# The sample attention of a decoder step written anew: keys turned by VectorE, running sums, unrolled units

## What is computed

```python
z = jnp.einsum('bqhd,bkhd->bhqk', qb, kb, preferred_element_type=jnp.float32) * scale + bias
log_beta = jax.nn.log_sigmoid(z)
log_keep = jnp.where(mask, log_beta - z, 0.0)
rest = lax.cumsum(log_keep, axis=3, reverse=True) - log_keep
a = jnp.where(mask, jnp.exp(log_beta + rest), 0.0)
outs.append(jnp.einsum('bhqk,bkhd->bqhd', a.astype(vb.dtype), vb))
```

## Time and profile before

| | |
|---|---|
| median of 3 runs | 3729.41 us (3727.08 to 3733.83) |
| the profiled execution | 3737.79 us |
| its span, first to last instruction | 3736.1 us |
| mean granted clock of PE | 0.946 |
| PE busy | 3210.8 us (86%) |
| DVE busy | 1885.8 us (50%) |
| ACT busy | 937.8 us (25%) |
| POOL busy | 610.8 us (16%) |
| DMA packets | 432.70 MB, mean 116 GB/s |

### The profile page before, as it was taken

One profiled execution on the slowest core, in us unless ns is written; L12 is line 12 of the kernel. 1 busy time (PEld: TensorE's weight loads), 2 busy tenths in 40 slices (PEclk: granted clock), 3 DMA queues, 4 the chain that ended last, 5 costly groups with the idle time before them and its releaser, 6 DMA issues. The chain is left out here.

```text
span 3736.1 us, 57991 instructions
## 1 busy us (share of the span) xinstructions
PE 3210.8 (86%) x20912; PEld 2718.3 (73%) x20912; DVE 1885.8 (50%) x3138; ACT 937.8 (25%) x1598; POOL 610.8 (16%) x528
## 2 busy tenths in 40 slices
PE   5655999999995979788888887888885999999997
PEld 1235999999985979555555555444484999999996
DVE  2566555555543121344444444888815555555554
ACT  0113000000012010333333333777714100000003
POOL 0002222212101111122222221000010222222210
PEclk7887999999997989899999998999997999999998
DMA  8702111111101220798888886000010211111101
GB/s 323 261 29 62 46 45 45 40 43 42 39 0 58 88 63 26 284 351 341 337 350 334 340 339 225 22 19 23 6 45 0 68 45 45 45 45 45 45 22 48
DMA packets 215604, 432.70 MB, mean 116 GB/s; under 512 B 13664, under 2 KB 130057, under 8 KB 212441
## 3 DMA queue, kind: packets, MB, share of 16 engines
q1 hardware_dynamic: 215521, 431.67, 31.7%
HBM read 417.92 MB, written 13.92 MB: 116 GB/s over the span
## 5 line engine op out<-in xcount | busy, mean ns | idle before, releaser
L84 PE MATMUL bank<-hi,mlp_uphi 128*128 128x364 f32 (+1 forms) x1536 | 506.9, 330 | 92.2 <-POOL mlp_uplo L697 92.2
L85 PE MATMUL bank<-lo,mlp_uphi 128*128 128x364 f32 (+1 forms) x1536 | 506.7, 330 | 0.0
L86 PE MATMUL bank<-hi,mlp_uplo 128*128 128x364 f32 (+1 forms) x1536 | 506.6, 330 | 0.0
L85 PE MATMUL bank<-mlp_flo,mlp_dnhi 128*128 128x364 f32 (+1 forms) x1536 | 504.7, 329 | 0.0
L86 PE MATMUL bank<-mlp_fhi,mlp_dnlo 128*128 128x364 f32 (+1 forms) x1536 | 504.7, 329 | 0.0
L84 PE MATMUL bank<-mlp_fhi,mlp_dnhi 128*128 128x364 f32 (+1 forms) x1536 | 504.6, 329 | 0.0
L307 DVE SCALAR_TENSOR_TENSOR x_t<-bank,mod,x_t 128x364 f32<-128x364 f32 (+1 forms) x432 | 245.5, 571 | 379.7 <-PE bank L86 377.4
L84 PEld LDWEIGHTS bank<-hi,mlp_uphi 128*128 128x128 f32 x1536 | 290.5, 189 | 93.4 <-POOL mlp_uplo L697 93.4
L697 POOL TENSOR_TENSOR mlp_uplo<-mlp_raw,mlp_uphi 128x1024 fp32r<-128x1024 f32 x64 | 162.5, 2540 | 827.3 <-ACT mlp_uphi L682 423.3
L85 PEld LDWEIGHTS bank<-lo,mlp_uphi 128*128 128x128 f32 x1536 | 290.5, 189 | 0.0
L86 PEld LDWEIGHTS bank<-hi,mlp_uplo 128*128 128x128 f32 x1536 | 290.3, 189 | 0.0
(11 more groups left out here) (255 smaller groups left out, 5652.7 us busy)
## 6 DMA issues: line engine op xcount, KB each, us to landing
sa_kpage<-in_cache_k SPq DMA_DIRECT2D x256, 512.0 KB, 6.4
sa_vpage<-in_cache_v SPq DMA_DIRECT2D x256, 512.0 KB, 6.1
mlp_raw<-in_w_up SPq DMA_DIRECT2D x64, 512.0 KB, 4.0
mlp_raw<-in_w_down SPq DMA_DIRECT2D x64, 512.0 KB, 3.5
w_raw<-in_w_ada SPq DMA_DIRECT2D x24, 1024.0 KB, 8.6
pm_wada<-in_w_ada SPq DMA_DIRECT2D x48, 512.0 KB, 5.2
kv_raw<-in_w_kv SPq DMA_DIRECT2D x8, 1024.0 KB, 5.5
x_rows<-in_x_prompt SPq DMA_DIRECT2D x1, 4096.0 KB, 13.4
```

The costliest lines, as they stand in the source:

```text
L84: pe.matmul(out, w_hi, x_hi, start=start, stop=False, skip_group_check=True)
L85: pe.matmul(out, w_hi, x_lo, start=False, stop=False, skip_group_check=True)
L86: return pe.matmul(out, w_lo, x_hi, start=False, stop=stop, skip_group_check=True)
```

## The change

The 64 units of the 8 sequences are counted through as n = 0 to 63 and unrolled, without a hardware loop.

- Keys are turned by DVE, in 32x32 blocks and from SBUF to SBUF, one instruction a page. It does so two units ahead: the four turns of unit n+2 stand at the head of DVE's iteration n, and the softplus chain of unit n behind them.
- The scores are made by 128 matmuls a unit with 32x32 weights and 128 columns at 16 positions of the array, into four banks by row group.
- ACT, and no longer DVE, adds the bias: four activations.
- DVE keeps a running sum of the softplus over the pages (sa_crun) and splits that. Six matmuls a unit with neg_tri and neg_above subtract it; neg_ones goes.
- POOL only prepares each sequence's share of the new keys. The queries of the next sequence are laid out in units 2 to 5, and a sequence is finished in the next one's unit 1. The output has two banks.
- SP's waits count turned pages by unit. Its order is as before. The first two units of keys are let through at the stage's start.
- setup makes two constants fewer (neg_ones, mask_diag: four POOL operations), and places move.

```diff
@@ attend_sample: sync
-sp.wait_ge(k_turned, b * TURNS + (2 * (n + 25) if n < 8 else 2 * (n - 7) + TURNS))
+sp.wait_ge(turned, b * (4 * UNITS) + (4 * u - 4 + EARLY_K))
-    sp.wait_ge(v_used, b * UNITS + (u + 6))
+    sp.wait_ge(v_used, b * UNITS + (u - 2 + EARLY_V))
@@ attend_sample: scalar
+def softplus_of_negative(n):
+    act.wait_ge(z_done, n + 1)
+    act.wait_ge(zt_done, n)
+    for r in range(4):
+        act.activation(z_rows[:, :, r, :],
+                       Z[r][:, P * (n % 2):P * (n % 2) + P].rearrange("p (x j) -> p x j", j=32),
+                       ACT.Identity, bias=k.bias_row[:, 0:1]).then_inc(z_kept, 1)
+    act.wait_ge(zt_done, n + 1)
+    act.wait_ge(c_done, 4 * n)
+    act.activation(flat, ZT[n % 2][:, :], ACT.Abs).then_inc(abs_done, 1)
+    act.wait_ge(abs_done, n + 1)
+    act.activation(flat, flat, ACT.Exp, scale=-1.0).then_inc(e_done, 1)
+    act.wait_ge(e_done, n + 1)
+    act.activation(flat, flat, ACT.Ln, bias=1.0).then_inc(l_done, 1)
+
+softplus_of_negative(0)
+for n in range(W):
+    if n + 1 < W:
+        softplus_of_negative(n + 1)
+    act.wait_ge(tri_done, n + 1)
+    if n:
+        act.wait_ge(v_used, EARLY_V + n)
+    act.activation(att[:, :, :].rearrange("p g n -> p (g n)"), ZT[n % 2][:, :], ACT.Exp).then_inc(a_done, 1)
@@ attend_sample: vector
+dve.tensor_reduce(sp_all[:, :], sp_new[:, :, :].rearrange("p b n -> p n b"), AX.X, ALU.add).then_inc(summed, 1)
...
+dve.tensor_reduce(att_all[:, :], att_new[:, :, :].rearrange("p b n -> p n b"), AX.X, ALU.add
+                  ).then_inc(summed, 1)
...
+def turn_keys(n, x):
+    if n >= W:
+        return
+    if x == 0:
+        if n >= 2:
+            dve.wait_ge(z_done, n - 1)
+    dve.wait_ge(k_in[4 * (n % 2) + x], 16 * (n // 2 + 1))
+    dve.transpose(k_t[n % 2][:, x, :], k_raw[n % 2][:, x, :]).then_inc(turned, 1)
...
+for n in range(2):
+    for x in range(4):
+        turn_keys(n, x)
+for n in range(W):
+    b, u = divmod(n, UNITS)
+    for x in range(4):
+        turn_keys(n + 2, x)
+    flat = t[:, :, :].rearrange("p g n -> p (g n)")
+    dve.wait_ge(l_done, n + 1)
+    dve.scalar_tensor_tensor(flat, ZT[n % 2][:, :], 0.0, flat, ALU.max, ALU.add).then_inc(sp_done, 1)
+    dve.wait_ge(sp_done, n + 1)
+    if n:
+        dve.wait_ge(lo_done, n)
+    for g in range(4):
...
+        dve.tensor_tensor(c_run[:, g, :], before, t[:, g, :], ALU.add).then_inc(c_done, 1)
+    c_all = c_run[:, :, :]
+    dve.wait_ge(c_done, 4 * n + 4)
+    if n:
+        dve.wait_ge(tri_done, n)
+    dve.tensor_copy(c_hi[:, n % 2, :, :], c_all).then_inc(hi_done, 1)
+    dve.wait_ge(hi_done, n + 1)
+    dve.tensor_tensor(c_lo[:, n % 2, :, :], c_all, c_hi[:, n % 2, :, :].bitcast(F32), ALU.subtract
+                      ).then_inc(lo_done, 1)
+    if u == 1 and b:
+        finish(b - 1)
+    if 2 <= u < 6 and b + 1 < DB:
+        ready_queries(b + 1, u - 2)
@@ attend_sample: tensor
+def scores(n):
+    b = n // UNITS
+    pe.wait_ge(turned, EARLY_K + 4 * n + 4)
+    if n >= 2:
+        pe.wait_ge(z_kept, 4 * (n - 1))
...
+    for hh in range(4):
+        for half in range(2):
+            for r in range(4):
+                for g in range(4):
+                    d0 = HD * (4 * g + hh) + 32 * half
+                    last = pe.matmul(
+                        Z[r][32 * g:32 * g + 32, P * (n % 2):P * (n % 2) + P].rearrange("p (x j) -> p x j", j=32),
+                        q_w[b % 2][32 * r:32 * r + 32, g, half, 32 * hh:32 * hh + 32],
+                        k_t[n % 2][32 * r:32 * r + 32, :, d0:d0 + 32],
+                        start=(hh == 0 and half == 0), stop=(hh == 3 and half == 1),
+                        tile_position=(32 * r, 32 * g), skip_group_check=True)
+    last.then_inc(z_done, 1)
...
+def subtract_sums(n):
...
+    pe.wait_ge(lo_done, n + 1)
...
+    for half, new in ((c_hi, pn_hi), (c_lo, pn_lo)):
+        pe.matmul(zt, k.neg_tri[:, :], half[:, n % 2, :, :], start=False, stop=False, skip_group_check=True)
+        pe.matmul(zt[:, 1:4, :], k.neg_above[:, :], half[:, n % 2, 0:3, :], start=False, stop=False,
+                  skip_group_check=True)
+        last = pe.matmul(zt[:, 0, :], k.neg_above[:, :], half[:, 1 - n % 2, 3, :] if u else new[:, :],
+                         start=False, stop=(half is c_lo), skip_group_check=True)
+    last.then_inc(tri_done, 1)
...
+scores(0)
+turn_scores(0)
+for n in range(W):
+    if n:
+        values(n - 1)
+    if n + 1 < W:
+        scores(n + 1)
+        turn_scores(n + 1)
+    subtract_sums(n)
+values(W - 1)
```

More of the change, by code:

```diff
@@ L965, in attend_sample @@
[L965 to L969, removed]
+        k_raw = [k.at(f"sa_kraw{s}", [P, 4, D], F32, o + 16384 * s) for s in range(2)]
+        k_t = [k.at(f"sa_kt{s}", [P, 4, D], F32, o + 32768 + 16384 * s) for s in range(2)]
+        kn_t = k.at("sa_knt", [P, NC, P], F32, o + 32768)
@@ L980, in attend_sample @@
[L980 to L994, removed]
+        z_rows = k.at("sa_zrows", [P, 4, 4, 32], F32, o + 32768)
@@ L1037, in _ @@
             pool.memset(v_new[:, :], 0.0).then_inc(zeroed, 1)
[L1038 to L1075, removed]
+            for s in range(2):
+                pool.memset(q_w[s][:, :, :, :], 0.0).then_inc(q_zeroed, 1)
@@ L1091, in _ @@
             act.activation(att_new[:, :, :].rearrange("p b n -> p (b n)"), zn[:, :], ACT.Exp).then_inc(an_done, 1)
[L1092 to L1107, removed]
-                    act.activation(t[:, :], ZTS[u % 2][:, :], ACT.Abs).then_inc(act_own, 1)
-                    act.wait_ge(act_own, b * (2 * UNITS) + (2 * u + 1))
-                    act.activation(t[:, :], t[:, :], ACT.Exp, scale=-1.0).then_inc(act_own, 1)
-                    act.wait_ge(act_own, b * (2 * UNITS) + (2 * u + 2))
-                    act.activation(t[:, :], t[:, :], ACT.Ln, bias=1.0).then_inc(t_done, 1)
-                weights(UNITS - 1)
@@ L1117, in _ @@
             new = Tally(dve, dve_new)
+            dve.sem_inc(turned, EARLY_K)
             dve.wait_ge(kn_turned, 2)
@@ new lines, in finish @@
+            def finish(b):
+                dve.wait_ge(v_used, EARLY_V + UNITS * (b + 1))
+                own = OA[b % 2][:, 4 * HD:8 * HD]
+                dve.tensor_tensor(own.rearrange("p (h d) -> p h d", h=4),
+                                  OA[b % 2][:, 0:4 * HD].rearrange("p (h d) -> p h d", h=4),
+                                  over(k.block_of[:, :], HD), ALU.mult).then_inc(o_part_done, 1)
+                dve.wait_ge(o_part_done, b + 1)
+                dve.tensor_reduce(o_rows[:, b, :], own.rearrange("p (h d) -> p d h", h=4), AX.X, ALU.add
+                                  ).then_inc(o_row, 1)
@@ new lines, in add_values, with values @@
+            def add_values(b, weight, v, start, stop):
+                for q in range(4):
+                    last = pe.matmul(OA[b % 2][32 * q:32 * q + 32, 0:4 * HD], weight[:, 32 * q:32 * q + 32],
+                                     v[:, 256 * q:256 * q + 256], start=start, stop=stop,
+                                     tile_position=(0, 32 * q), skip_group_check=True)
+                return last
+            def values(n):
+                b, u = divmod(n, UNITS)
+                if u == 0:
+                    pe.wait_ge(new_ready, 2 * b + 2)
+                    pe.wait_ge(vn_in, 16)
+                    if b >= 2:
+                        pe.wait_ge(o_part_done, b - 1)
+                    add_values(b, att_b, v_new, True, False)
+                pe.wait_ge(a_done, n + 1)
+                for g in range(4):
+                    slot = 4 * (n % 2) + g
+                    pe.wait_ge(v_in[slot], 16 * (n // 2 + 1))
+                    last = add_values(b, att[:, g, :], v_page[:, slot, :], False, u == UNITS - 1 and g == 3)
+                last.then_inc(v_used, 1)
```

274 lines of the change are left out of this document (105 added, 169 removed).

## The result

The changed kernel takes 4002.1 us (median of 4 runs, 3995.3 to 4005.3); the kernel before took 3728.3 on the same chip (4 runs). The ratio is 1.0729, 95% interval 1.071 to 1.0747. The forecast was 3645, with a range up to 3765. The profiled execution took 4001.7 us, its span is 3999.9.

A forecast was written before the change was run, and what follows sets the result against it. Page DMA was to bound the sample attention at 10.3 us a unit; half the slow-clock cost made it 11.0. Then 1537.7 + 61 x 11.0 + 16 ends the stage 84.8 us earlier: 3645 us, range 3598 to 3765.

The forecast's parts named there:

- rival 4: Code loading: PE's unrolled code takes DMA engine time, 1.3 to 2.0 us more for a unit's pages; 3700 us, chance 0.07.
- Unrolling removes the drain: PE's loop drains between sequences, each costing 98.8 us instead of 91.1; unrolled code was to end that.
- no gap each 8th unit: Sign that the forecast is right: in the stage, no pause at the end of each sequence of 8 units.
- The ring of value slots: Value loads wait for v_used, behind key turns and chain: two units take 8.4 + 2.1 + 10.3 us, 10.4 each.
- Transpose: DVE's key turn of one 128x1024 page, taken as one pass: 1.23 us, four a unit.
- DVE's chain: The softplus chain on DVE: max-and-add, four running sums, cast, subtraction and waits, 3.3 us a unit.
- DMA's floor: Loading a unit's 8 pages of 512 KB at 406 GB/s takes at least 10.3 us, 660 us for the stage.
- Scores: On PE, 256 load-and-multiply pairs a unit, 16 positions at once, 7 ns a pair: 2.1 us with tail.
- rival 1: PE's scores issue or run slower than 16 at a time, deciding from 23 ns a pair; 3740 to 3800 us, chance 0.13.
- The ring of the scores: Exponential, values, scores, bias, turned scores, three activations and waits in sequence: 8.5 us a unit at full clock.
- The head: Start of the stage: two reductions of 1.2 us precede DVE's first key turn, at 1525.6; early key pages cost nothing.
- rival 3: PE's clock stays at half: 12.4 us a unit, 3729 us, no change; chance 0.08.

The follow-up runs named there:

- sp_order: Changed kernel with SP issuing the next sequence's key pages 0 ahead of this sequence's last value pages: 3934.8 us, ratio 1.0536 to the kernel before.
- full_loop: Changed kernel with SP's order made the same across sequences and PE's whole stage as one loop over a two-unit body: 3731.9 us, ratio 1.0001.
- full_loop_chain_first: The fastest version: changed kernel with PE's stage looped over two units, SP's order the same across sequences and DVE's softplus chain ahead of key turns: 3652.0 us, ratio 0.9779.
- straight_chain_first: Changed kernel, PE's code still straight, with SP's order the same across sequences and DVE's chain ahead of the key turns: 3942.5 us, ratio 1.0562.
- body_of_four: The fastest version (3652 us) with four units instead of two in PE's loop body, run half as often: 3983.7 us, ratio 1.067.
- half columns: The two-unit-loop kernel of 3731.9 us, with seven of the scores' eight rounds multiplying 64 of 128 columns (scores not right): 3743.3 us, ratio 1.0027.

## Why the prediction was wrong, step by step

**The step that failed** is rival 4, code loading: it was seen, but as 0.65 us a packet taken from one DMA engine, 1.3 to 2.0 us a unit added to the pages. The price is not the DMA engine's time but PE's: a block can be used 6.0 us after PE has gone into the one before, and PE goes through 128 undisturbed pairs in 1.7 us. 2.34 packets a unit at one each 6.25 us (the median between packets in the stage) are 14.6 us a unit, by themselves more than any ring of the prediction. That more doesn't come of it was argued from a loop's first pass, the full stretch in the earlier trace rows; there the packets come 14 to 20 us apart, more than twice the 6.0 us. The rival had 0.07 and 3700 us; it should have been costed per instruction: what does PE do in the 6 us. Worth here: from sp_order to full_loop 5.35%, 200 us; with DVE's chain ahead of the turns the loop is worth 292 to 332. The Trainium skill's "mostly hidden" (Runtime: NRT & Kernel Launch, Instruction fetch mechanics) fails for this kernel. The same section says that kernels prefer full unrolling where possible; here that points the wrong way, by these 200 us.

**"Unrolling removes the drain", "no gap each 8th unit": wrong.** SP was not unrolled. Its order at a sequence's end cost seven steps of 10 us; by sp_order 1.93%, 72 us.

**The ring of value slots: right in kind, 3.3 us short for two units** (24.1 for 20.8). The missing terms: SP's own issues ahead of the keys (0.7), the pages' landing (1.1), and the stretch from the last landing (9.9 for 8.4), in which the sums stand behind the turned scores and the clock is low. It counts only where the chain is behind the turns: 2.22%, 83 us.

The three parts, 72 for SP's order, 200 for the code and 83 for the turns, are steps of one path from the changed kernel to the fastest, so they add up to its 355 us by themselves. On another path each has another size: the turns are worth nothing while the code is straight.

**That the fastest version ends near the 3645 of the forecast is in part luck.** Its last values end at 2225.1, where 2224.7 was forecast, but the forecast had 11.0 us a unit, 0.6 of it for a low clock, and the units without a gap have 10.28 at 0.98, some 44 us less in all. Against that stand 18 us more in the first sequence and 8 in the last, where new code comes in, and a first turn 6 us later.

**Terms that held.** Transpose 1.24 (1.23). DVE's chain 3.1 (3.3). Bias 1.14 (1.1), turned scores 0.66 (0.6), sums 1.23 at full clock (1.2), values 1.93. DMA's floor of 10.3 us and 406 GB/s: 403 GB/s over 560 us in the fastest version. The 358 GB/s that the Trainium skill gives as a core's share (DMA: Bandwidth & Descriptors, Specifications) are passed here, where one core runs alone, over 11 times the stretch of the earlier trace rows.

**Terms that didn't.** Scores 3.58 for 2.1: 13.0 ns a pair, where 7 was taken and 23 was the point of decision, so rival 1 fell. So does the 25 ns from start to start of the Trainium skill (TensorE: Matmul & The Clock Gate, Part 1), for pairs of different positions: 9.7 ns were measured with 64 columns. The ring of the scores is 9.87 us (forecast 8.5), nearly all of it these 1.5; it hid under DMA's 10.3. The head: DVE's first turn came at 1529.8, not 1525.6: 16 query copies (3.4 us) stand ahead of it, and each reduction takes 1.9, not 1.2.

**Clock (rival 3).** It is 0.70 in the stage, between its two levels, and it follows the gaps: full_loop has 0.87, full_loop_chain_first 0.98, while straight_chain_first and body_of_four stay at 0.71 and 0.74. So it is no separate cause; what part of the 200 us it makes was not measured apart.

## What to carry to other kernels

Count instructions as a resource. Where an engine issues 256 short ones in less time than a block of code takes to come (here 3.7 us with idle and 6.0 us with full DMA engines), straight code is bound by its own loading, and a wait released by "issue" at steps of 128 load-and-multiply pairs is its mark; keep the busy engine in a loop that fits (1,210 instructions did, 2,420 did not); the other engines' code could stay unrolled here. When one engine is unrolled, look for the loop that stays (here SP's order of issues). And price an edit again after the bound is gone: beside SP's new order the same edit of DVE was worth nothing with straight code, then 83 us.

## What was not expected of the hardware

- A packet of 16 KB takes 1 us, but PE goes on only 1.4 us after its landing, with or without page traffic; and it starts 3.7 us after PE has gone on under page traffic, 1.2 without. At all 63 gaps no packet starts between the landing and PE going on, and the next starts 1.1 to 5.1 us after. So it seems to be asked for only when PE enters the block before; no row shows the asking.
- A loop that doesn't fit is worse than straight code: 199 packets for 187, 3984 us for 3942 with the same orders.
- Pairs of 32x32 weights and 128 columns at 16 positions start 13.0 ns apart, with 64 columns 9.7.
- Less work on PE came with a kernel slower by 0.26% (half columns) and a clock of 0.77 for 0.87.
